# Another order of the tensors in a partition of SBUF: the low parts of the rounded weights begin 32 bytes past a multiple of 128

## The reference

```
h = h + 0.5 * SwiGLU_1(RMSNorm(h))            # 1024 -> 2816 -> 1024
u = RMSNorm(h);  z = u @ w_in                 # q, k, v of three attentions, forget logits, three gates
m = sum_i sigmoid(gate_i) * (o_i @ proj_i)    # differential, forgetting and stick-breaking attention
h = h + m @ w_out
h = h + 0.5 * SwiGLU_2(RMSNorm(h))
```

## Time and profile before

| | |
|---|---|
| three runs | 2423.38, 2423.43, 2424.64 us |
| the profiled execution, its own time | 2424.2 us |
| its span, first to last instruction | 2422.0 us |
| PE (matmul) busy | 2411.1 us, 15594 matmuls |
| PEld (weight load) busy | 2223.9 us |
| DVE, ACT busy | 2120.6 us, 1499.2 us |
| granted TensorE clock | 0.999 |

### The profile page before, as it was taken

The page is one execution under the profiler, slowest core; times in us unless marked ns, Lnnn a source line. Parts: engine busy times, 40 slices in busy tenths (PEclk is TensorE's granted clock), DMA queues, the critical chain, the costliest instruction groups (busy, mean ns, idle before and its releaser), DMA issues.

```text
span 2422.0 us, 48244 instructions
## 1 busy us (share of the span) xinstructions
PE 2411.1 (100%) x15594; PEld 2223.9 (92%) x15594; DVE 2120.6 (88%) x3964; ACT 1499.2 (62%) x2948; POOL 3.2 (0%) x10
## 2 busy tenths in 40 slices
PE   9999999999999999999999999999999999999999
PEld 8999888999889889998889998889998998899988
DVE  8999878999898779998699997789998986899986
ACT  6666448888754456664366663578886554566643
POOL 0000000000000000000000000000000000000000
PEclk9999999999999999999999999999999999999999
DMA  4333322212232323333323333322212332233332
GB/s 163 109 105 104 114 95 71 71 61 78 62 114 88 105 87 109 104 105 117 108 93 109 105 99 105 114 70 62 70 62 71 105 114 97 92 109 105 111 114 79
DMA packets 64675, 233.46 MB, mean 96 GB/s; under 512 B 7168, under 2 KB 7552, under 8 KB 64512
## 3 DMA queue, kind: packets, MB, share of 16 engines
q1 hardware_dynamic: 64368, 231.32, 29.3%
q10 hardware_dynamic: 144, 0.11, 0.0%
HBM read 229.30 MB, written 2.10 MB: 96 GB/s over the span
## 4 chain that ended last, share of the span: by engine, by line
PE 94%; DVE 3%; ACT 1%; issue 1%; DMA 0%; DVEq 0%; ACTq 0%
PE ps L754 27%; PE ps L755 27%; PE ps L756 27%; PE ps L1005 3%; PE ps L1074 2%; PE ps L1056 2%; PE ps L1057 2%; PE ps L1058 2%; PE ps L1028 2%; DVE w_lo L2085 1%; ACT area L1338 1%; DVE area L2085 0%; ACT w_hi L1338 0%; DVE u_lo L2105 0%; DVE scratch_whole L2111 0%
## 5 line engine op out<-in xcount | busy, mean ns | idle before, releaser
L1338 ACT ACTIVATE w_hi<-w_raw 128x512 fp32r<-128x512 f32 (+2 forms) x888 | 623.9, 713 | 478.3 <-PE ps L756 220.5
L2085 DVE TENSOR_TENSOR w_lo<-w_raw,w_hi 128x512 fp32r<-128x512 f32 (+2 forms) x888 | 699.4, 796 | 104.9 <-ACT w_hi L1338 88.5
L754 PE MATMUL ps<-u_hi,w_hi 128*128 128x256 f32 (+1 forms) x2240 | 708.3, 316 | 0.8 <-ACT scratch_whole L1444 0.8
L756 PE MATMUL ps<-u_hi,w_lo 128*128 128x256 f32 (+1 forms) x2240 | 705.8, 315 | 0.0
L755 PE MATMUL ps<-u_lo,w_hi 128*128 128x256 f32 (+1 forms) x2240 | 705.6, 315 | 0.0
L755 PE MATMUL ps<-area,w_hi 128*128 128x256 f32 (+1 forms) x1778 | 583.3, 328 | 0.0
L754 PE MATMUL ps<-area,w_hi 128*128 128x512 f32 (+1 forms) x1414 | 482.0, 341 | 1.1 <-ACT scratch_whole L1444 0.9
L756 PE MATMUL ps<-area,w_lo 128*128 128x512 f32 (+1 forms) x1414 | 480.1, 340 | 0.0
L754 PEld LDWEIGHTS ps<-u_hi,w_hi 128*128 128x128 f32 x2240 | 427.3, 191 | 27.7 <-DVE w_lo L2085 1.5
L756 PEld LDWEIGHTS ps<-u_hi,w_lo 128*128 128x128 f32 x2240 | 427.1, 191 | 26.8
L755 PEld LDWEIGHTS ps<-u_lo,w_hi 128*128 128x128 f32 x2240 | 427.3, 191 | 25.8
(11 more groups left out here) (208 smaller groups left out, 3153.8 us busy)
## 6 DMA issues: line engine op xcount, KB each, us to landing
w_raw<-weights SPq DMA_DIRECT2D x432, 512.0 KB, 3.7
h<-x SPq DMA_DIRECT2D x4, 512.0 KB, 6.4
out<-scratch_whole SPq DMA_DIRECT2D x8, 256.0 KB, 2.0
scratch_whole<-const_b SPq DMA_DIRECT2D x1, 256.0 KB, 9.0
scratch_whole<-const_r SPq DMA_DIRECT2D x1, 192.0 KB, 8.4
cst<-const SPq DMA_DIRECT2D x1, 143.0 KB, 8.0
par<-params ACTq DMA_DIRECT2D x1, 105.0 KB, 4.4
```

What stands on the lines that cost most here:

```text
L754: pe.matmul(dst, hi, x_hi, start=start, stop=False, **kw)
L756: return pe.matmul(dst, lo, x_hi, start=False, stop=stop, **kw)
L1338: return act.activation(dst, src, ACT.Copy)
L2085: return dve.tensor_tensor(dst, src, hi_part.bitcast(F32), ALU.subtract)
```

## The change

The order of the tensors in a partition is another one. No instruction, wait or loop is changed.

```diff
-        cst = sb("cst", C_END)
-        masks = sb("masks", MASK_ZEROS + NQ * P, BF16)
-        par = sb("par", P_END)
-        stat = sb("stat", 24)
-        sb("gap1", 8)
-        base = sb("base", SEQ, F16)
-        ones_r = sb("ones_r", P, F32R)
         h = sb("h", ND * SEQ)
         u_hi = sb("u_hi", ND * SEQ, F32R)
...
         area_whole, area = sb_two("area", AREA)
+        masks = sb("masks", MASK_ZEROS + NQ * P, BF16)
+        lam = sb("lam", 16)
+        sb("gap1", 8)
         w_hi = sb("w_hi", W_COLS, F32R)
-        sb("gap2", 112)
+        par = sb("par", P_END)
+        stat = sb("stat", 24)
+        sb("gap2", 8)
         w_lo_whole, w_lo = sb_two("w_lo", W_COLS)
-        lam = sb("lam", 16)
+        base = sb("base", SEQ, F16)
+        ones_r = sb("ones_r", P, F32R)
+        cst = sb("cst", C_END)
```

## The result

Seven runs of the changed kernel have a median of 2431.48 us (2430.72 to 2432.31), seven of the kernel before 2423.65 (2423.38 to 2425.07): 7.8 us slower, ratio 1.003 (95% interval 1.002 to 1.0039). The profiled execution took 2430.72 us, its span is 2428.5, 6.5 more than before.

The account below looks back on a forecast made before the run. The matmuls' spacing on TensorE was taken to bound the kernel. Nearly all terms were 0: 2424.2 + 0.3 us for the profiled execution, 2423.6 us against the runs' median, range 2404 to 2436 us.

Parts of the forecast that it names:

- within 0.2%: Whole kernel: time within about 5 us of the kernel before, chance 0.56.
- rival B: Loads of w_lo before 256-column matmuls outgrow their cover: 12 us slower, 2436, or 53 us, 2477; chance 0.19.
- the fixed 13 ns: Time between matmul streams, read as equal for 256 and 512 columns; one ns on all 15594 matmuls is 16 us.
- part 5: w_raw as target of the DMA loads, and tokens and weights now differing in phase by 384 bytes: taken as 0.
- part 1: 3108 loads of w_lo before 256-column matmuls, now 32 bytes past a multiple of 128: 0 us, 5 us without slack.
- A: Gaps between matmuls shrink on a third of the 256-column ones, 113 ns for 120: 2402 us, half 2413; chance 0.22.
- The 113 ns: A distance between 256-column matmuls just after 512-column ones, read as showing that less than 120 ns is possible.
- The row on the streaming side: 392-column matmuls starting 32 or 64 bytes past a multiple of 128, read as 1.7 to 3.3 ns slower than aligned.
- C: VectorE's unaligned writes slow it beyond its 4% of slack: at 5% about 8 us lost, 2432; chance 0.05.
- parts 3 and 4: VectorE's writes of w_lo: nothing, up to 2 us hidden; moved constants and small tensors: 0 us, at most 1.3.
- the 4%: VectorE's slack in 256-column stretches, from 95.87 us busy in a 100 us window.

Follow-up runs that it names:

- m1: TensorE alone on constant data, 66 settings of operand places, no other engine at work: equal places 120.0 and 226.8 ns, the changed kernel's 118.2 and 233.3 ns.
- m3: TensorE alone, w_hi and w_lo at all 256 pairs of places in steps of 16 bytes, twice in random orders: 80 pairs differed by over 0.6 ns between passes.
- e8: The changed kernel with gaps altered so that w_hi and w_lo stand as the tokens do by 256 bytes: 2424.11 us, ratio 1.0003.
- e5: The kernel before with 64 bytes of gap ahead of w_hi, so w_hi and w_lo both stand 64 bytes past the tokens by 256: 2419.7 us.
- e7: The kernel before with w_hi 192 and w_lo 64 bytes by 256 past the tokens: 2432.83 us, ratio 1.0039.
- e9: The kernel before with w_hi and w_lo both 240 bytes by 256 past the tokens: 2420.07 us, ratio 0.9989.
- e1 to e4: The changed kernel with w_lo back at a multiple of 128: 2433.8 us; the kernel before with w_lo 32, 64, 96 bytes further: 2432.58, 2421.06, 2434.98 us.
- e10: The kernel before with w_hi 192 and w_lo 96 bytes by 256 past the tokens: 2410.7 us, ratio 0.9947.

## Why the prediction was right and wrong

The measured 2431.48 us lies in the range of 2404 to 2436, but "within 0.2%" was the likeliest case, and the result is outside it (7.8 us, 0.3%). That the range held is luck: its upper end was the 2436 us of rival B, a mechanism that did not occur, and the measured time is the remainder of two terms of which one had been put at nothing.

**What bounds the kernel** was read rightly: the spacing of matmuls. The last sentence of the prediction named the weak point, that "the fixed 13 ns depends on where two operands lie". It does.

**The step that failed** is part 5 of the change, phases against one another, with "I take 0", and with it part 1. The argument was that 256 and 512 columns pay the same 13 ns over their streaming, so it is a fixed cost of changing over. It is the value of one placement. In the changed kernel the excess is 11.1 ns for 256 columns (117.8 - 106.7) and 20.1 for 512 (233.4 - 213.3); in m1 to m3 it runs from 6.6 to 18 for 256 (from 113.3 to 124.7 ns) and from 13 to some 22 for 512. One placement had been all that the trace showed of it, and I said so, but gave it too little weight. The priced terms were -22 to +5 us for the 256-column ones and nothing for the 512-column ones; measured -17 and +25. The gain would have been 2.2 x 9324 = 20.5 us by the rhythm alone; some 3 us of it went in longer waits in the long stretches. That a longer stream would be the one to lose, with all its cover for the load, no case of mine had.

**Rivals.** A had the sign and nearly the size for 256 columns: 6.6 ns a triple instead of 7, of which 4.1 lie ahead of L756 and the rest in the other two distances, where it had them all at L756. It had nothing for 512 columns. The 113 ns that it leaned on was misread: the starts of the earlier trace rows to the nanosecond give 113, then 119, so it is the first distance after the turn from 512 columns, with `w_hi` in both matmuls, and not the one ahead of L756. B had the right sign of the whole and 2436 us for a time, by a wrong road: under 256 columns L756 came sooner, 115.9 ns after L755 and not later than 120, and the 512-column ones did not "stay at 227". The row on the streaming side that B and part 1 rested on the earlier trace rows could not show the effect: to the nanosecond k = 1 and 2 are 1.0 and 2.0 ns a matmul above k = 3, not 1.7 and 3.3, and in the second pass over the same columns, from 375.56 us on, it is -0.3 and +0.2. C was wrong: 688, 953 and 1221 ns for the writes of `w_lo`, and 2.5 us of waits for them.

The Trainium skill, SBUF — State Buffer, section Specifications (TRN2), was cited with its 16-byte lines, by which 32 bytes off touch no line more. No run here shows the line, and whole lines did not decide: in m1 `w_lo` moved by 32 bytes, two such lines, took 120.0 to 118.5 and 226.7 to 233.2 ns, and of the shifts in that sweep only 256 brought both back.

**Right:** parts 3 and 4, and of part 5 the DMA, by e8: 0.7 us with an interval that holds zero. That VectorE stands close behind TensorE in the 256-column stretches was right too, but its slack is less than the 4% read from its busy time: the long stretches went from 120.4 to 118.6 ns at best, which is 1.5%.

## What to carry to other kernels

Where matmuls run back to back, each with its own weight load, look at the distance of starts for each width, and do not take its excess over the streaming for a constant. Here it hung on where stationary and streaming operands stand against one another by 256 bytes: try a few gaps, read both widths separately, since a total near zero can be two large terms, and distrust a good value that a second pass in another order does not repeat. Once TensorE is quicker, the engine behind it takes part of the gain: in e5 a rhythm 5.6% shorter gave 1.5% where VectorE was 96% busy, and all of it where VectorE was 89% busy. So weigh a placement by the stretches in which TensorE is free to use it.

## What the runs showed of the hardware

- The distance between fp32r matmuls with alternating weights varied with the placement of SBUF operands by up to 10% (113.3 to 124.7 ns at 256 columns), with TensorE the only engine at work. The effect repeats every 256 bytes and stays when all places move together. Transposes of 128 columns, each with its own load, stayed at 109 ns in every placement tried. What inside the chip makes the effect stays open; no run here takes it apart.
- With all places equal, 256 columns were at 120.0 ns in every setting and 512 at 226.7 to 228.2. Other pairs were mostly shorter for 256 (mean of m3's grid 118.2) and longer for 512 (231.9).
- Some placements have two or more rhythms, and which one runs goes with what ran before: 113.3 or 118.8 ns for one pair. So a bare measurement need not carry over to the kernel (e7, and e9 in the long stretches), though before, the change and e1 to e4 agree with it within 0.5 ns, and e5, e9 and e10 within 0.1 ns in the short stretches.
